# Opening of a two-layer encoder trunk: the first two chunks of the first up product taken together, by pairs of depths

## The reference

```python
x = layer_norm(ALPHA * x + 0.5 * swiglu_ffn(x, ffn1_w_up[l], ffn1_w_down[l]), ln1_g[l], ln1_b[l])
mix = hybrid_mixer(x, ...)          # state-space branch and sparse attention, gated and merged
x = layer_norm(ALPHA * x + mix, ln2_g[l], ln2_b[l])
x = layer_norm(ALPHA * x + 0.5 * swiglu_ffn(x, ffn2_w_up[l], ffn2_w_down[l]), ln3_g[l], ln3_b[l])

def swiglu_ffn(x, w_up, w_down):
    gate, up = jnp.split(x @ w_up, 2, axis=-1)
    return (jax.nn.silu(gate) * up) @ w_down
```

## Time and profile before

| what | us |
|---|---|
| median of 3 runs | 1100.02 |
| lowest, highest | 1099.73, 1100.76 |
| profiled execution, own time | 1100.38 |
| its span | 1098.5 |
| PE busy in the span | 1090.3 |
| DVE busy | 796.9 |
| ACT busy | 590.5 |

### The profile page before, as it was taken

The page is one execution under the profiler, slowest core; times in us unless marked ns, Lnnn a source line. Parts: engine busy times, 40 slices in busy tenths (PEclk is TensorE's granted clock), DMA queues, the critical chain, the costliest instruction groups (busy, mean ns, idle before and its releaser), DMA issues.

```text
span 1098.5 us, 18341 instructions
## 1 busy us (share of the span) xinstructions
PE 1090.3 (99%) x6377; PEld 926.5 (84%) x6377; DVE 796.9 (73%) x1102; ACT 590.5 (54%) x850; POOL 367.8 (33%) x441
## 2 busy tenths in 40 slices
PE   9999999999999999999999999999999999999997
PEld 8888888998788888888888888889877888888886
DVE  6686866789878867686677566477897787656644
ACT  6565533574873556463345555336858645645530
POOL 3998971108700289993200000011284000000000
PEclk9999999999999999999999999999999999999999
DMA  9876673743665595667466666636545666666641
GB/s 288 263 228 225 232 232 114 230 119 128 175 214 192 178 291 180 190 216 239 130 209 192 206 211 205 210 90 210 168 132 158 202 200 215 193 204 210 208 161 39
DMA packets 159551, 211.09 MB, mean 192 GB/s; under 512 B 12952, under 2 KB 107640, under 8 KB 159488
## 3 DMA queue, kind: packets, MB, share of 16 engines
q1 hardware_dynamic: 155360, 202.56, 58.5%
q10 hardware_dynamic: 2688, 3.44, 1.3%
q0 software_dynamic: 1440, 4.27, 1.2%
HBM read 209.11 MB, written 1.10 MB: 191 GB/s over the span
## 4 chain that ended last, share of the span: by engine, by line
PE 99%; DVE 0%; DVEq 0%; issue 0%
PE ps L846 24%; PE ps L788 17%; PE ps L789 17%; PE ps L790 17%; PE ps L850 12%; PE ps L1185 2%; PE ps L1187 1%; PE ps L1188 1%; PE ps L859 1%; PE ps L802 1%; PE ps L1053 1%; PE ps L1071 1%; PE ps L1100 1%; PE ps L1121 1%; PE ps L1111 1%; PE ps L1279 0%
## 5 line engine op out<-in xcount | busy, mean ns | idle before, releaser
L1307 DVE TENSOR_TENSOR wlo<-raw,whi 128x1024 fp32r<-128x1024 f32 (+1 forms) x367 | 478.6, 1330 | 121.3 <-ACT whi L450 118.4
L450 ACT CAST whi<-raw 128x1024 fp32r<-128x1024 f32 (+1 forms) x367 | 377.2, 1042 | 233.2 <-PE ps L790 157.2
L846 PE MATMUL ps<-x_hl,whi 128*128 128x512 f32 x1152 | 362.5, 396 | 0.1
L850 PEld LDWEIGHTS ps<-x_hl,wlo 128*128 128x128 f32 x1152 | 216.4, 188 | 51.1
L850 PE MATMUL ps<-x_hl,wlo 128*128 128x256 f32 x1152 | 226.5, 278 | 0.0
L1770 POOL TENSOR_TENSOR rstd<-var_eps,cst 128x1 f32<-128x1 f32 x11 | 16.8, 1528 | 531.0 <-DVE var_eps L1375 531.0
L846 PEld LDWEIGHTS ps<-x_hl,whi 128*128 128x128 f32 x1152 | 175.7, 189 | 0.6 <-issue 0.3
L788 PE MATMUL ps<-whi,x_hl 128*128 128x512 f32 (+1 forms) x400 | 156.6, 392 | 0.0
L789 PE MATMUL ps<-wlo,x_hl 128*128 128x512 f32 (+1 forms) x400 | 153.1, 383 | 0.0
L790 PE MATMUL ps<-whi,x_hl 128*128 128x512 f32 (+1 forms) x400 | 153.1, 383 | 0.0
L788 PE MATMUL ps<-whi,hh 128*128 128x512 f32 (+1 forms) x355 | 138.0, 389 | 0.0
(11 more groups left out here) (203 smaller groups left out, 1357.8 us busy)
## 6 DMA issues: line engine op xcount, KB each, us to landing
raw<-in_ffn_w_up SPq DMA_DIRECT2D x352, 256.0 KB, 3.9
raw<-in_ffn_w_down SPq DMA_DIRECT2D x176, 256.0 KB, 3.3
raw<-in_w_in SPq DMA_DIRECT2D x128, 256.0 KB, 3.5
raw<-in_w_branch SPq DMA_DIRECT2D x32, 256.0 KB, 3.3
raw<-in_w_out SPq DMA_DIRECT2D x32, 256.0 KB, 3.7
bias_g<-bias_rows ACTq DMA_DIRECT2D x16, 192.0 KB, 3.9
raw<-in_w_in SPq DMA_DIRECT2D x16, 148.0 KB, 2.3
affine<-in_ln_g SPq DMA_DIRECT2D x4, 512.0 KB, 5.7
```

The source lines that it names most:

```text
L450: nc.scalar.copy(whi[:, s % RING, 0:w], raw[:, s % RAW, 0:w]).then_inc(S["hi_done"], 1)
L846: nc.tensor.matmul(ps[:, bank, :], w(whi, s + q, at, at + P), x_hl[:, k, :, :], start=k == 0, stop=False)
L850: ins = nc.tensor.matmul(ps[:, bank, 0:SEQ], w(wlo, s + q, at, at + P), xh[:, k, :], start=False, stop=k == KT - 1)
L1307: nc.vector.tensor_tensor(wlo[:, s % RING, 0:w], raw[:, s % RAW, 0:w], f32(whi[:, s % RING, 0:w]), ALU.subtract).then_inc(S["split_done"], 1)
```

## The change

Chunks 0 and 1 are made together. Even slots 0, 2, 4, 6 now hold chunk 0, odd slots 1, 3, 5, 7 chunk 1; slot s holds the depths of pair s // 2. PE fills banks 0 and 1 from even slots and banks 2 and 3 from odd ones, so all four banks grow side by side. x is loaded and split one pair of depths for every two slots. Slots 0 to 3 are loaded and split in halves, slots 4 to 7 whole (slot 4 was in halves before). For slots 4 to 7 PE takes each depth's three products token tile by token tile, behind a wait for the low part. ACT and DVE now take slots 8 to 11 ahead of the silus of chunk 0, and slot 12 between the silus of chunk 0 and those of chunk 1, as before; slots 13 to 15 stay behind. The second silu of chunk 0 waits for slot 6 to be used.

```diff
@@ wait_up
-            eng.wait_ge(S["pe_used"], used(s + 4))
+            eng.wait_ge(S["pe_used"], used(7) if f == 0 and c == 0 else used(s + 4))
@@ SP
-            def load_depths(q, w):
-                for k, landed in ((2 * q, half_landed[q % RAW]), (2 * q + 1, raw_landed[q % RAW])):
...
+            def load_opening(w):
+                for s in range(2 * RAW):
+                    d, c = s // 2, s % 2
+                    if c == 0 and d > 0:
+                        load_columns(d)
+                    if s < RAW:
+                        for k, landed in ((2 * d, half_landed[s]), (2 * d + 1, raw_landed[s])):
+                            dst = raw[:, s, depth(k)].rearrange("p (g n) -> p g n", g=2)
+                            sp.dma_start(dst, w[0, :, k, :, c, :]).then_inc(landed, 16)
+                    else:
+                        dst = raw[:, s % RAW, :].rearrange("p (t g n) -> p t g n", t=2, g=2)
+                        load(0, s, [(dst[:, :, g], w[0, :, 2 * d:2 * d + 2, g, c, :]) for g in range(2)])
+                sp.dma_start(ident[:, :], A["ident"]).then_inc(S["ident_landed"], 16)
@@ ACT token_chunk
-                if f == 0 and c == 1:
-                    split_hi(0, s + RING)
+                if f == 0:
+                    for q in range(4 if c == 0 else 1):
+                        split_hi(0, s + RING + q)
                 for t in range(NT):
                     wait_up(act, f, s, c, t)
...
                     if t == (1 if f == 0 else 0):
-                        for q in range(1 if f == 0 and c == 1 else 0, 4):
+                        for q in range((4 if c == 0 else 1) if f == 0 else 0, 4):
                             split_hi(0, s + RING + q)
@@ ACT, ahead of the first block
+            for s in range(RAW):
+                for k in (s // 2 * 2, s // 2 * 2 + 1):
+                    if s % 2 == 0:
+                        columns_hi(k)
...
+            for s in range(RAW, 2 * RAW):
+                if s % 2 == 0:
+                    columns_hi(s)
+                    columns_hi(s + 1)
+                split_hi(0, s)
@@ PE opening
+                def product(a, ring, s, k, t, stop=False):
+                    return nc.tensor.matmul(ps[:, 2 * (s % 2) + t, :], a[:, k, tok(t)], ring[:, s, depth(k)],
+                                            start=k == 0 and a is xh and ring is whi, stop=stop)
...
+                def by_token(s, k):
+                    if s % 2 == 0:
+                        pe.wait_ge(S["cols_lo"], k + 1)
+                    wait_lo(s, k)
                     for t in range(NT):
+                        product(xh, whi, s, k, t)
+                        product(xl, whi, s, k, t)
+                        ins = product(xh, wlo, s, k, t, stop=k == KT - 1)
+                        if t == 0 and k == KT - 1:
                             ins.then_inc(S["up_done"], 1)
+                    return ins
+                for s in range(2 * RAW):
+                    for k in (s // 2 * 2, s // 2 * 2 + 1):
+                        ins = by_kind(s, k) if s < RAW else by_token(s, k)
+                    ins.then_inc(S["pe_used"], 1)
```

More of the change, by code:

```diff
@@ L368, in load_columns @@
                 sp.dma_start(x_cols[:, 2 * q:2 * q + 2, :], A["x_t"][q]).then_inc(cols_landed[q + 1], 16)
-            def load_depths(q, w):
-                for k, landed in ((2 * q, half_landed[q % RAW]), (2 * q + 1, raw_landed[q % RAW])):
-                    dst = raw[:, q % RAW, depth(k)].rearrange("p (g n) -> p g n", g=2)
-                    sp.dma_start(dst, w[0, :, k % KT, :, k // KT, :]).then_inc(landed, 16)
+            def load_opening(w):
[11 more added lines that the diff above has]
+                sp.dma_start(ident[:, :], A["ident"]).then_inc(S["ident_landed"], 16)
             def ffn(l, which, n, s0):
@@ L378, in ffn @@
                 for c in range(PEEL):
[L379 to L388, removed]
+                    if n == 0 and c < OLD_C:
+                        if c == 0:
+                            load_opening(w_up)
                     else:
@@ L445, in split_hi @@
                 w = width(s)
-                act.wait_ge(raw_landed[s % RAW], 32 * (2 * i + s // RAW) + (16 if s % RAW else 0))
+                act.wait_ge(raw_landed[s % RAW], 32 * (2 * i + s // RAW) + 16)
                 if s >= RING:
@@ L759, in _ @@
                 act.dma_start(x_cols[:, k, :], A["x_t"][0, :, k, :]).then_inc(cols_landed[k], 16)
[L760 to L770, removed]
+            for s in range(RAW):
+                for k in (s // 2 * 2, s // 2 * 2 + 1):
+                    if s % 2 == 0:
+                        columns_hi(k)
+                    if k % 2 == 0:
+                        act.wait_ge(half_landed[s], 16)
+                        nc.scalar.copy(whi[:, s, depth(k)], raw[:, s, depth(k)]).then_inc(S["half_hi"], 1)
+                    else:
+                        act.wait_ge(raw_landed[s], 16)
+                        nc.scalar.copy(whi[:, s, depth(k)], raw[:, s, depth(k)]).then_inc(S["hi_done"], 1)
+            for s in range(RAW, 2 * RAW):
[3 more added lines that the diff above has]
+                split_hi(0, s)
             for l in range(DEPTH):
@@ L863, in wait_hi @@
+                def wait_hi(s, k):
                     if k % 2 == 0:
-                        pe.wait_ge(S["half_hi"], k // 2 + 1)
+                        pe.wait_ge(S["half_hi"], s + 1)
                     else:
[L866 to L870, removed]
-                    else:
[L872 to L876, removed]
+                        pe.wait_ge(S["hi_done"], s + 1)
@@ L877, in opening, with wait_lo, by_kind @@
+                def wait_lo(s, k):
+                    if s >= RAW or k % 2 == 1:
+                        wait_split(s)
+                    else:
+                        pe.wait_ge(S["half_lo"], s + 1)
+                def by_kind(s, k):
+                    if s % 2 == 0:
+                        pe.wait_ge(S["cols_hi"], k + 1)
+                    wait_hi(s, k)
                     for t in range(NT):
-                        product(xh, whi, k, t, start=k == 0)
-                    pe.wait_ge(S["cols_lo"], k + 1)
+                        product(xh, whi, s, k, t)
+                    if s % 2 == 0:
+                        pe.wait_ge(S["cols_lo"], k + 1)
@@ L880, in opening @@
                     for t in range(NT):
-                        product(xl, whi, k, t)
-                    wait_lo(k)
+                        product(xl, whi, s, k, t)
+                    wait_lo(s, k)
                     for t in range(NT):
[L884 to L902, removed]
@@ L904, in opening @@
-                for k in range(2):
-                    wait_lo(KT + k)
-                    for t in range(NT):
[L907 to L916, removed]
-                            ins.then_inc(S["up_done"], 1)
+                        ins = product(xh, wlo, s, k, t)
@@ new lines, in by_kind @@
+                    return ins
+                def by_token(s, k):
+                    if s % 2 == 0:
+                        pe.wait_ge(S["cols_lo"], k + 1)
+                    wait_lo(s, k)
+                    for t in range(NT):
+                        product(xh, whi, s, k, t)
+                        product(xl, whi, s, k, t)
+                        ins = product(xh, wlo, s, k, t, stop=k == KT - 1)
+                        if t == 0 and k == KT - 1:
+                            ins.then_inc(S["up_done"], 1)
+                    return ins
@@ L1328, in token_chunk @@
             def token_chunk(f, s, c):
-                if f == 0 and c == 1:
-                    split_lo(0, s + RING)
+                if f == 0:
+                    for q in range(4 if c == 0 else 1):
+                        split_lo(0, s + RING + q)
                 for t in range(NT):
@@ L1714, in columns_lo @@
                                         ).then_inc(S["cols_lo"], 1)
[L1716 to L1723, removed]
+            for s in range(RAW):
+                for k in (s // 2 * 2, s // 2 * 2 + 1):
+                    if s % 2 == 0:
+                        columns_lo(k)
+                    dve.wait_ge(S["half_hi" if k % 2 == 0 else "hi_done"], s + 1)
+                    nc.vector.tensor_tensor(wlo[:, s, depth(k)], raw[:, s, depth(k)], f32(whi[:, s, depth(k)]),
+                                            ALU.subtract).then_inc(S["half_lo" if k % 2 == 0 else "split_done"], 1)
+            for s in range(RAW, 2 * RAW):
+                if s % 2 == 0:
+                    columns_lo(s)
+                    columns_lo(s + 1)
+                split_lo(0, s)
             for l in range(DEPTH):
```

## The result

The changed kernel takes 1105.11 us in the median (6 runs, 1102.93 to 1106.38), the kernel before 1100.37 (6 runs, 1099.73 to 1100.76). The ratio is 1.0041 with a 95% interval of 1.0030 to 1.0052. Note the spread too: 3.45 us between the runs of the changed kernel, 1.0 before. The profiled execution took 1105.77 with a span of 1104.0, 5.5 us more than the span of before. (Further down, one run of experiment 4 and one of experiment 6 took 3.5 times and twice as long as all others; they are left out of the medians and ranges.)

What follows compares the result with a forecast made beforehand. PE, busy for 1090.3 of 1098.5 us, was taken as the bound, so any wait is paid in full. Chunk 2's late start, taken as +2.5, on the median of 1100.0 gave 1102.5, range 1101.1 to 1104.0.

Steps and rivals of the forecast that it cites:

- the late start: Chunk 2's first weight load goes at 29.77 instead of 27.21, +2.56 us, taken as +2.5 and carried to the end.
- rival E: PE's clock falls in the stall ahead of chunk 2, losing 2.1 us on top: 1104.6; chance 0.06.
- Steps 3 to 5: From slot 11's cast through table load, silus and products to chunk 2's first weight load: 3.65 us in sum.
- Step 1: Slot 7's cast on ACT starts at 18.82, as before.
- Step 2: Slot 11 reuses slot 7's raw buffer; a turn takes 7.3 us, so slot 11's cast starts at 26.12.
- rival B: Slot 11 lands as late as before, so chunk 2 starts +3.4 us late: 1103.4; chance 0.2.
- the bound from above: Upper limit on chunk 2's delay: with slot 11's cast at 26.97 as before, PE goes at 30.62, +3.4.
- Rival D: Table load stands ahead of the four casts, shortening the chain to chunk 2 by 1.29: +1.3, 1101.3; chance 0.07.
- its one gap: PE's 0.21 us wait ahead of 8.24 in the opening would close, gaining 0.2 us that only lengthens the next wait.
- signs of being wrong: Chunk 2's first weight load near 27.2, PE waiting in the opening for slots 4 to 7, or a stall without later end.
- the low part of slot 4: In the opening, wanted whole at 16.2 and ready at 15.9, 0.3 us early; up to 0.5 late costs nothing.
- The drain: About 1380 ns per table switch on ACT; would lengthen the stall by 1.4 us to +3.9, left out of the sum.

Runs made afterwards that it cites:

- experiment 4: Changed kernel with one silu of a single column ahead of ACT's first cast, so the table is loaded at the start; 1104.41 us, ratio 1.0040.
- experiment 6: Changed kernel with no cast of slots 8 to 11 ahead of chunk 0's silus, the order of the kernel before; 1101.89 us, ratio 1.0017.
- experiment 2: Changed kernel with chunk 0's silus and products behind slots 8 and 9 and ahead of slots 10 and 11; 1100.48 us, ratio 1.0003.
- experiment 3: Kernel before, not interleaved, with only the ACT and DVE order changed: slots 8 to 11 ahead of chunk 0's silus; 1104.19 us, ratio 1.0036.
- experiment 5: Changed kernel with chunk 0's silus behind the casts of slots 8 to 10 and slot 11 behind them; 1101.76 us, ratio 1.0015.
- experiment 8: Changed kernel with 11 warm-up matmuls on PE between the opening and the wait ahead of chunk 2; 1103.38 us, ratio 1.0028.
- experiment 1: Changed kernel once more, no edit, for a second profile, timed against the kernel before; 1105.53 us, ratio 1.0053.
- experiment 7: Changed kernel with 6 warm-up matmuls on PE between the opening and the wait ahead of chunk 2; 1103.20 us, ratio 1.0034.
- experiment 9: Kernel before with only the ACT and DVE order changed, plus 11 warm-up matmuls in its stall; 1102.95 us, ratio 1.0023.

## Why the prediction was wrong

- **The mechanism was right.** The silus stand behind slot 11's cast, PE waits for them, and nothing gives it back. Experiments 2, 3 and 5 show it: the loss follows the cast that is last ahead of the silus, with the interleaving or without it.
- **The step that failed: that the time is the late start alone, and rival E at a chance of 0.06.** I argued for the clock from 40 slices that all show the upper level. But these hold no idle piece like the one that I predicted, so they said nothing about it. It fell in 8 of 11 runs, by their mean granted clock. What it costs is the step from the changed kernel to the one with 11 matmuls in the stall: +4.5 and +5.8 (the two ratios) less +3.1 (0.0028 of 1100.25), so 1.4 to 2.7 us; 1.55 us in the profile shown (1.65 less the 0.1). The size that rival E gave it, 2.1, was about right by luck: it took the length of the slow stretch from the warm-up, 4.21 us, for which no row spoke, and the stretch was 3.4 us. Without this term the median, at about +3.1, would lie inside the range of 1101.1 to 1104.0; it lies beyond it by this term.
- **The term that was mis-sized: the late start, +2.5.** It is about +3.1 by experiment 8. In the seven profiles with four casts ahead of the silus (experiments 1, 3, 4, 7, 8, 9 and the first one) chunk 2's first weight load is 2.7 to 4.0 us late, 3.1 in the median. Steps 3 to 5 were right: 3.65 forecast, 3.60 measured. Steps 1 and 2 were not. Step 1 had slot 7's cast at 18.82 "as before"; with the new order of loads it is at 19.88 and 19.23 in the changed kernel's two profiles, and at 19.01 to 19.88 in all eight profiles that have this order. Step 2 took 7.3 for the turn of the buffer. It was 7.76 and 7.05 in these two, and 7.55 to 8.14 in the other five of the seven. The rows had warned of it: step 2 left out slot 6 to slot 10, 17.41 to 25.58, a second turn of 8.17. So slot 11's cast came at 26.28 to 27.64, 26.89 in the median, which is where rival B had it (26.97), at a chance of 0.2. B's cause isn't needed for it: SP's queue has an issue of 1.02 to 2.09 us, of slot 10 or 11, in five of the seven, but none in the first profile, whose turn was 7.76. Nor was +3.4 the bound from above that the prediction took it for: the first profile's slot 11 came 0.67 us later still.
- **Rival D's price.** With the table load out of the way it had steps 3 to 5 shorter by 1.29. Experiment 4 shows 0.55, for DVE's low part of slot 11 comes next.
- **The opening.** I expected its one gap to close. In the first profile there were three, because slot 0's first half is cast at 4.71 (4.57 before), slot 1's at 7.99 (wanted done by 8.05) and slot 4 at 14.88 (forecast 13.6); in the second profile one of 0.47, for slot 4. So one of the prediction's signs of being wrong, PE waiting inside the opening for slot 4, did come, in a small size. From issue to landing the half slots issued in the first 4.6 us took 3.8 to 6.1 us in the first profile and 3.6 to 5.3 in the second, against 3.8 to 4.9 before. Why they take longer with less of x between them is left open; no run takes it apart. The order of work does lose here: the low part of slot 4 has 0.3 us of slack on paper and is late by about half a us in both. As forecast, this drops out of the sum where the stall follows: in experiment 2, where none follows, 0.7 us at chunk 2's first matmul are left, and 0.4 in the span.
- **Table load.** It starts 0.02 us after the cast ends (27.64 + 1.05, then 28.71) and the silu comes 0.01 after it, as in the earlier trace rows. The drain that the Trainium skill adds to a load in "ScalarE: Activation LUTs", What ACT_TABLE_LOAD costs, doesn't show here either, and leaving it out was right.

## What to carry to other kernels

Before moving the reader of a PSUM bank behind other work on its engine, follow the last item ahead of it back to what that one waits for: here a transfer, which had nothing to do with the bank. For the time of such a transfer take all turns that the rows show, the long ones too. Before taking an item out of a chain, look for what stands next to it on another engine. Where PE is busy for the whole span and a change opens a gap of 2 us or more, count the gap and the slower work behind it, and expect a wide spread of the runs. If the gap can't be avoided, matmuls whose result nobody reads can fill it: 11 of them took 1.2 to 2.2 us off the medians here. What they cost themselves is some tenths at most: with them the changed kernel took 1102.86 to 1103.75, and 1102.50 to 1103.35 in its three runs in which the clock stayed up.

## What the runs showed of the hardware

- **A gap of PE of 2.1 to 2.8 us mostly halves the granted clock.** In profiles with gaps of 2.8, 2.8 and 2.1 us ahead of chunk 2 (changed kernel, order only, table early) it fell to one half, for 3.4 us in the first and third and 6.8 in the second; behind one of 2.3 us (the changed kernel again) it did not, nor behind 1.0 and 1.1 (experiments 7 and 5). So the length alone doesn't decide it. Nor does the fall come in the gap alone: in order only it came at about 29.6, with PE idle since 27.4, but in the first and third about 0.8 us after PE had started again (32.1 against 31.27, and 31.1 against 30.32). The Trainium skill, "TensorE: Matmul & The Clock Gate", Part 1, says that the gate's window runs freely and does not start with the kernel. That one unchanged program shows the fall in 8 of 11 runs would fit that; no run here shows the phase itself.
- **The granted clock of the first microseconds isn't what the matmuls show.** The warm-up matmuls take 4.21 us for 18 at the start, 234 ns each, and 2.62 us for 22 in experiment 8, 119 ns each: half. The page of the profile gives both stretches the upper level. The pace at the start is what the lower one would give; no run here shows that the clock is the reason.
